# Attention scores from block-diagonal keys, the pass flag ahead of the gather, and a reordered last group of down steps, in a one-core Trainium2 step of a hybrid decoder layer

## What is computed

```python
def token_mix(x, ...):
    h = rmsnorm(x, g_mix)
    mq, mk, mv, mo, mi, mf, aq, ak, av = split_in(h @ w_in)
    # 4 mLSTM heads (256 x 256 memory), and 16 query heads on 4 key heads of 64,
    # sliding window of 128, with a sink per head
    return x + concatenate([o_m, o_a]) @ w_out, states

def sink_attention(q, k, v, allowed, sinks):
    s = einsum('...thgd,...khd->...hgtk', q, k) * 64 ** -0.5
    s = where(allowed, s, -inf)
    mx = maximum(max(s), sink)
    e = exp(s - mx)
    p = e / (sum(e) + exp(sink - mx))
    return einsum('...hgtk,...khd->...thgd', p, v)

def channel_mix(x, p_i, ...):
    # top-1 of 4 groups, top-2 of 8 experts in it, 32 SwiGLU experts of 512
    x = x + hier_moe(rmsnorm(x, g_ffn), ...)
    gate = sigmoid(rmsnorm(x, g_ple) @ w_ple_gate)
    return x + gate * (p_i @ w_ple_proj)
```

## Time and profile before, and how to read it

| what | us |
|---|---|
| median of 3 executions | 1517.54 |
| lowest, highest | 1515.83, 1518.03 |
| profiled execution, its own time | 1517.73 |
| its span | 1516.0 |
| PE busy | 1364.2 (90%) |
| weight loads busy | 859.7 (57%) |
| DVE, ACT, POOL busy | 350.8, 252.4, 31.4 |
| DMA, mean | 348 GB/s |

### The profile page before, as it was taken

The page is one execution under the profiler, slowest core; times in us unless marked ns, Lnnn a source line. Parts: engine busy times, 40 slices in busy tenths (PEclk is TensorE's granted clock), DMA queues, the critical chain, the costliest instruction groups (busy, mean ns, idle before and its releaser), DMA issues.

```text
span 1516.0 us, 22808 instructions
## 1 busy us (share of the span) xinstructions
PE 1364.2 (90%) x9764; PEld 859.7 (57%) x9765; DVE 350.8 (23%) x938; ACT 252.4 (17%) x558; POOL 31.4 (2%) x69
## 2 busy tenths in 40 slices
PE   9989999999999999987978787888788888999986
PEld 7878888888888543433523333333333356666655
DVE  3312221036621411301301010101010112222217
ACT  3201121041401322111101111110111111101015
POOL 1000000020022000000000000000000000000000
PEclk9999999999999999989989899899998999999998
DMA  9556333377978699999999999999999999999981
GB/s 343 204 169 227 118 132 113 138 279 264 375 291 371 268 427 401 426 427 428 426 427 428 428 429 429 428 429 428 428 429 428 429 413 427 426 426 428 427 345 58
DMA packets 64640, 527.50 MB, mean 348 GB/s; under 512 B 6030, under 2 KB 27926, under 8 KB 29350
## 3 DMA queue, kind: packets, MB, share of 16 engines
q1 hardware_dynamic: 63182, 525.27, 84.5%
q10 hardware_dynamic: 1384, 1.16, 0.2%
HBM read 512.33 MB, written 14.07 MB: 347 GB/s over the span
## 4 chain that ended last, share of the span: by engine, by line
DMA 42%; PE 26%; DVE 1%; issue 1%; ACT 1%; DVEq 0%; ACTq 0%
DMA raw<-in_w_up 26%; DMA more<-in_w_up 8%; PE ps L1944 7%; DMA raw<-in_w_down_cuts 7%; PE ps L2208 4%; PE ps L2182 4%; PE ps L154 4%; DMA more<-in_w_down_cuts 1%; PE ps L2192 1%; PE ps L1184 1%; PE ps L1968 1%; PE ps L1919 1%; PE ps L1957 1%; PE ps L1260 1%; PE ps L1239 0%
## 5 line engine op out<-in xcount | busy, mean ns | idle before, releaser
L154 PE MATMUL ps<-mixT_hT,raw 128*128 128x264 f32 x1920 | 436.1, 387 | 2.3 <-PEq L808 1.7
L154 PEld LDWEIGHTS ps<-mixT_hT,raw 128*128 128x128 f32 x1920 | 361.9, 190 | 67.1 <-issue 6.9
L1944 PE MATMUL ps<-raw,mixT_hT 128*32 128x512 f32 x1488 | 200.2, 669 | 90.7 <-DMA raw<-in_w_up 62.0
L1944 PEld LDWEIGHTS ps<-raw,mixT_hT 128*32 128x32 f32 x1488 | 43.0, 116 | 212.6 <-DMA raw<-in_w_up 88.3
L2208 PE MATMUL ps<-mixT_hT,more 128*128 128x264 f32 x512 | 126.1, 395 | 1.2 <-ACT mixT_hT L2289 1.2
L1199 DVE TENSOR_TENSOR mixT_hT<-ps,ffn_gain 128x512 f32<-128x512 f32 x33 | 22.8, 691 | 417.9 <-PE ps L1919 417.9
L2208 PEld LDWEIGHTS ps<-mixT_hT,more 128*128 128x128 f32 x512 | 94.9, 191 | 30.8 <-issue 16.4
L1184 PE MATMUL ps<-x_res,mine 128*32 128x512 f32 (+1 forms) x792 | 109.0, 668 | 0.0
L1957 PEld LDWEIGHTS ps<-fold,mixT_hT 128*128 128x128 f32 x512 | 69.3, 210 | 53.6 <-issue 35.2
L1919 PEld LDWEIGHTS ps<-ident,xe 128*64 128x64 f32 x1056 | 66.5, 217 | 28.3 <-issue 28.3
L1957 PE MATMUL ps<-fold,mixT_hT 128*128 128x32 f32 x512 | 76.6, 296 | 5.7 <-ACT mixT_hT L1766 5.7
(11 more groups left out here) (373 smaller groups left out, 905.5 us busy)
## 6 DMA issues: line engine op xcount, KB each, us to landing
raw<-in_w_gate SPq DMA_DIRECT2D x62, 2048.0 KB, 16.5
raw<-in_w_down_cuts SPq DMA_DIRECT2D x35, 2048.0 KB, 17.5
more<-in_w_up SPq DMA_DIRECT2D x32, 2048.0 KB, 15.4
raw<-in_w_up SPq DMA_DIRECT2D x31, 2048.0 KB, 16.9
raw<-in_mix_chunks SPq DMA_DIRECT2D x60, 1024.0 KB, 5.4
more<-in_w_down SPq DMA_DIRECT2D x16, 2048.0 KB, 22.4
more<-in_w_down_cuts SPq DMA_DIRECT2D x13, 2048.0 KB, 25.6
more<-in_w_gate_cuts SPq DMA_DIRECT2D x8, 2048.0 KB, 21.6
```

Of the source, the lines that this page charges most:

```text
L154: return nc.tensor.matmul(ps[:, j, 0:NT], core.raw[:, q % NCH, k * GW + j * P:k * GW + (j + 1) * P], xT[:, core.groups[g].k0 + c * CK + k, ...
L1944: last = nc.tensor.matmul(ps[own, (GATE, UP)[m], :], xT[:, k, i * SLOTS:(i + 1) * SLOTS], weights, start=(i == 0 and k < 4), stop=(i == EI ...
```

## The change

In attention, `kswp` gives way to `both_keys`, two buffers (for even and odd `g`) of two rows of blocks: the keys of one key head in the upper 64 partitions with zeros below, and the same keys in the lower 64 with zeros above. One product of 128 rows takes the queries of two heads as weights and both key blocks as 2 x 128 or 2 x 256 columns; its output holds the scores of both heads. Two products per unit replace four. POOL clears the zero halves behind its other work (four memsets) and signals `a_clear`; DVE copies the keys of head 0 and 1 at the start and those of 2 and 3 behind units 1 and 3 (`group_keys`). PE waits for `a_clear` ahead of all scores, and for `a_keys` in each unit. In the routing, the sums for the flag (`before`) are made ahead of DVE's wait for the ranks, PE's counting product goes ahead of the gather and into bank 6, both pieces of `state(3, b)` go behind the gather, and the flag is made right behind `mine`. In finish_stage step 5 follows the order of the others, and `most_total` comes behind the last block.

```diff
-    kswp = S("kswp", [P, 2, NT])
+    both_keys = S("both_keys", [P, 2, 2, SEQ])
...
             pool.sem_inc(q["a_const"], 1)
+            for i in range(2):
+                link(nc.gpsimd.memset(both_keys[HD:P, i, 0, :], 0.0))
+                link(nc.gpsimd.memset(both_keys[0:HD, i, 1, :], 0.0))
+            pool.sem_inc(q["a_clear"], 1)
...
-            pe.wait_ge(q["a_swap"], 2)
+            pe.wait_ge(q["a_clear"], 1)
             pe.wait_ge(q["a_rows"], 2)
...
-                for i in range(4):
-                    h = 4 * g + i
-                    lo = (h % 2) * HD
-                    keys = pT[lo:lo + HD, AK0 + g // 2, 0:span(b)] if h % 2 == g % 2 else kswp[lo:lo + HD, g // 2, 0:span(b)]
-                    last = nc.tensor.matmul(ps[:, 4 + i % 2, (i // 2) * 256:(i // 2) * 256 + span(b)],
-                                            pT[lo:lo + HD, AQ0 + h // 2, b * P:(b + 1) * P], keys,
+                pe.wait_ge(q["a_keys"], 2 * g + 2)
+                for a in range(2):
+                    out = ps[:, 4 + a, :].rearrange("p (i c) -> p i c", i=2)[:, :, 0:span(b)]
+                    last = nc.tensor.matmul(out, pT[:, AQ0 + 2 * g + a, b * P:(b + 1) * P], both_keys[:, g % 2, :, 0:span(b)],
                                             start=True, stop=True)
...
-            nc.vector.tensor_copy(kswp[0:HD], pT[HD:P, AK0:AK0 + 2, :]).then_inc(q["a_swap"], 1)
-            nc.vector.tensor_copy(kswp[HD:P], pT[0:HD, AK0:AK0 + 2, :]).then_inc(q["a_swap"], 1)
+            def group_keys(g):
+                if g >= 2:
+                    dve.wait_ge(q["a_scores"], 2 * g - 2)
+                src = pT[g % 2 * HD:(g % 2 + 1) * HD, AK0 + g // 2, 0:SEQ]
+                for half in range(2):
+                    nc.vector.tensor_copy(both_keys[half * HD:(half + 1) * HD, g % 2, half, :], src).then_inc(q["a_keys"], 1)
+
+            group_keys(0)
+            group_keys(1)
...
                 if u % 2:
                     projected(u // 2)
+                    if u < 5:
+                        group_keys(u // 2 + 2)
...
+        pe.wait_ge(q["r_before"], 1)
+        nc.tensor.matmul(ps[:, 6, 0:NE], core.ones[:], before[:, 2, :], start=True, stop=True).then_inc(q["r_counted"], 1)
+        gather_slots(core, pe, rt, shared, 0)
         state(3, 0)
-        gather_slots(core, pe, rt, shared, 0)
         state(3, 1)
-        pe.wait_ge(q["r_before"], 1)
-        nc.tensor.matmul(ps[:, 0, 2 * P:2 * P + NE], core.ones[:], before[:, 2, :], start=True, stop=True).then_inc(q["r_counted"], 1)
...
+        dve.wait_ge(q["r_counted"], 1)
+        link(V.tensor_reduce(c[:, 8, 0:1], ps[:, 6, 0:NE], AX, ALU.max))
+        V.tensor_tensor(rt["flag"][:], c[0:1, 8, 0:1].to_broadcast([1, PASSES]), rt["level"][0:1, :], ALU.is_gt
+                        ).then_inc(shared["flag_ready"], 1)
...
-                elif j == GROUPS - 1:
-                    gates(c - 1, j)
-                    if c == LAST:
-                        most_total()
-                    down(c, j)
-                    sums(c, j)
                 else:
                     down(c, j)
                     gates(c - 1, j)
                     sums(c, j)
+        most_total()
```

More of the change, by code:

```diff
@@ L493, in attention @@
     st = S("st", [P, 4, NS])
-    names = ("a_const a_swap a_rows a_rowsT a_sinks a_win a_new a_stored a_scores a_shift a_exp "
+    names = ("a_const a_clear a_keys a_rows a_rowsT a_sinks a_win a_new a_stored a_scores a_shift a_exp "
              "a_prob a_turn a_turned a_pv a_mixed a_bias s_sinks s_q s_keysT s_kcopy s_scores s_shift s_exp s_turn "
@@ L726, in _ @@
                     src = ps[:, 4 + a, :].rearrange("p (i c) -> p i c", i=2)[:, :, 0:span(b)]
-                    nc.vector.scalar_tensor_tensor(sm[:, u % 2, a::2, 0:span(b)], src, HD ** -0.5, msk, ALU.mult, ALU.add
+                    nc.vector.scalar_tensor_tensor(sm[:, u % 2, 2 * a:2 * a + 2, 0:span(b)], src, HD ** -0.5, msk, ALU.mult, ALU.add
                                                    ).then_inc(q["a_shift"], 1)
@@ L1614, in vector @@
         link(V.tensor_tensor(c[:, 9, :], rt["pick_r"][:, 0:3, 0], rt["pick_r"][:, 3:6, 0], ALU.add))
+        link(V.tensor_tensor(before[:, 1, :], both[:, 0, :], both[:, 1, :], ALU.add))
+        link(V.scalar_tensor_tensor(before[:, 2, :], both[:, 2, :], valid[:], before[:, 1, :], ALU.mult, ALU.add))
+        dve.sem_inc(q["r_before"], 1)
         dve.wait_ge(q["r_ranked"], 1)
@@ L1620, in vector @@
         dve.sem_inc(shared["pick_step"], 1)
+        dve.wait_ge(q["r_counted"], 1)
+        link(V.tensor_reduce(c[:, 8, 0:1], ps[:, 6, 0:NE], AX, ALU.max))
+        V.tensor_tensor(rt["flag"][:], c[0:1, 8, 0:1].to_broadcast([1, PASSES]), rt["level"][0:1, :], ALU.is_gt
+                        ).then_inc(shared["flag_ready"], 1)
         ranks = ps[:, 0, P:P + 3 * NE].rearrange("p (o e) -> p o e", o=1).to_broadcast([P, 2, 3 * NE])
         link(V.tensor_tensor(taken.rearrange("p (i t) e -> p i (t e)", i=2), ranks, pick[:].rearrange("p i t e -> p i (t e)"), ALU.mult))
-        link(V.tensor_tensor(before[:, 1, :], both[:, 0, :], both[:, 1, :], ALU.add))
-        link(V.scalar_tensor_tensor(before[:, 2, :], both[:, 2, :], valid[:], before[:, 1, :], ALU.mult, ALU.add))
-        dve.sem_inc(q["r_before"], 1)
         link(V.tensor_reduce(rt["rank"][:], taken, AX, ALU.add))
@@ L1629, in vector @@
         V.tensor_tensor(c[:, 5, :], c[:, 4, :], c[:, 3, :], ALU.subtract).then_inc(q["r_in2"], 1)
[L1630 to L1633, removed]
         dve.wait_ge(shared["gain_landed"], 16)
```

## The result

The changed kernel took 1527.76 us (median of six, 1524.97 to 1530.83) against 1517.34 us (median of six) for the kernel before: a ratio of 1.007, 95% interval 1.006 to 1.008. It is 10.4 us slower. The forecast was 1519.5 us and its range ended at 1523.0, so it was wrong. The profiled execution took 1530.83 us, the slowest of the six, with a span of 1528.4 us against 1516.0, 12.4 more.

The account below looks back on a forecast made before the run. Prediction: DMA loads of expert weights bound the kernel from 574 us on; PE counts before that and after the last landing. Terms 3.8 + 0 + 1.4 - 0.8 - 2.0 - 0.4 = +2.0 us gave 1519.5 us, range 1516.5 to 1523.0.

Parts of the forecast that it names:

- Between 574 and 1464 us PE's time is hidden: From the restart of the weight-load stream to the last down step, PE's gains or losses do not move the end.
- a dry stretch of the stream behind 580 us: Sign of a wrong forecast: the load stream, expected full until the last down step, runs dry after 580 us.
- The price of the attention units, +3.8: Attention scores: two products of 512 columns replace four paired ones and cost 3.8 us more, bounds +3.2 and +4.4.
- Rival 3: Attention scores: half-zero products cost no more than paired halves and the drains go, 1.6 us gained, 1514.1 us; chance 0.07.
- Start of the stage, 0 and +1.4: Attention start: PE's wait for the clearing costs 0, the clock falling behind that idle time costs 1.4 us.
- Rival 2: Attention start: the clock holds behind the wait, so 1.4 us less, 1518.1 us; chance 0.17.
- Routing tail, -0.8: Routing tail: the flag's load runs beside the queued state products, so x_turn starts 0.8 us sooner.
- Clock in the routing, -2.0: Routing tail: without the 1.4 us hole the clock does not fall, 2.0 us gained, bounds 0 and -2.1.
- rival 1: Routing tail gives nothing back: flag load waits for state products, or the clock falls all the same; 1522.3 us, chance 0.20.
- End, -0.4: Last block: down ahead of gates lets the sums and everything behind them come 0.4 us sooner, bounds -0.7 and +0.5.

Follow-up runs that it names:

- e1: Changed kernel plus 25 TensorE instructions in a branch that is not run, moving the finish's code back; 1521.78 us, ratio to the kernel before 1.0039.
- e7: As e1, with the four clearings of the key tile ahead of the mask on GpSimd; 1520.00 us, ratio to the kernel before 1.0018.
- e8: Changed kernel without its attention part, so routing and finish only; 1515.80 us against 1517.25 for the kernel before, ratio 0.9994.
- e9: The kernel of e8 measured once more, nothing changed; 1516.70 us against 1517.87 for the kernel before, ratio 0.9994.
- e3: Attention part of the change alone on the kernel before; 1526.67 us, ratio 1.0069.
- e6: Changed kernel plus 8 TensorE instructions in the branch that is not run; 1528.49 us (one run).
- e5: Kernel before plus 199 TensorE instructions in the branch that is not run; 1524.11 us against 1517.25, ratio 1.0038.
- e10: Kernel of e8 with the branch for further passes left out of TensorE's program; 1515.56 us against 1517.87 for the kernel before, ratio 0.9986.
- e4: Routing part of the change alone on the kernel before; 1516.34 us, ratio 0.9996.

## Why the prediction was wrong, point by point

By medians: the place of the code 6.0 us (after less e1), the wait for the clearing with its clock 1.8 (e1 less e7), the block-diagonal units 3.8 (e7's 1520.00 less 1516.25, the middle of e8 and e9), routing and finish -1.3 (middle of e8 and e9). Together 10.3, where 10.4 were measured; since each term is the step from one kernel to the next, the sum is no test of them. The split is good to about 1 us: by means of the runs, each less the kernel before measured beside it, it is 4.8, 2.5, 4.2 and -1.1. The prediction had 0, 1.4, 3.8 and -3.2.

- **"Between 574 and 1464 us PE's time is hidden" is the step that failed.** It was read from a DMA share that stays full in the kernel before. The share says that no stop empties the stream now; it doesn't say how much more it bears. What the runs show in its place is +8.89 us in just this stretch, from a second stop that the prediction had no term for, since it never asked where the finish's code would lie. Its own sign of being wrong, a dry stretch of the stream behind 580 us, is what came (DMA share 0.30 from 1230 to 1235 us). TensorE already stood still for 4.87 us at 1213 us. From the restart to the first product of the finish, 643.1 us pass in e3 and 643.4 in e6, and the second stop costs 3.3 and 3.4 us of the stream's piece; in the changed kernel and e5 it is 647.1 and 647.2 us, and it costs 8.9 and 8.7. That being late raises the price fits these four executions and is not shown apart from them. Without a second stop 645.1 us cost nothing in e1 (877.91); e7, e8 and e9 took 1.7 to 2 us more in this piece (879.95, 879.70, 879.70), and that stays open. In the changed kernel part of the lateness is a stretch at half clock (0.62 and 0.69 in the windows 1205 to 1210 and 1210 to 1215 us).
- **The price of the attention units, +3.8: right.** The traces give 3.58, and 3.6 to 3.7 in all five kernels with this part; a unit with two key blocks takes 1.82 us, forecast 1.7 to 1.8. Rival 3 (a half-empty product costs no more) is out: the columns account for the price.
- **Start of the stage, 0 and +1.4: right in sum, by another split.** The clearing was done at 103.85 us, earlier than the 104.1 forecast, and the clock fell as feared. The first turn came 1.22 us later in this execution, 2.66 in e1's. Rival 2 (the clock holds) fell. In e7, with a wait of 1.67 us, it would have been right; in e10 the clock fell behind 1.50 us, so the wait alone doesn't decide it.
- **Routing tail, -0.8: the mechanism is right.** The register load does overlap: x_turn starts at 526.19, as the state's products end (524.27 + 1.99), where the earlier trace rows have 1.43 us of idle time ahead of it. The size is right too: at full clock the piece is 0.8 us shorter (134.8 against 135.61).
- **Clock in the routing, -2.0: mis-sized.** The first expert had its full clock (5.36 us), but the fall came earlier and hit the gather (4.55 in place of 2.91 us). The claim was that without the 1.4 us hole the clock would hold. It held in e5 with that hole (1.44 us) and fell in e4 without it. Over the kernels with the new routing the piece from 436 to 574 us takes 134.8 to 139.8 us (mean of eight 136.5); with the old one 135.6 to 137.6 (mean of four 137.0). So routing gave 0.5 us on the mean where 2.8 were forecast. That was the second half of rival 1.
- **End, -0.4: right where it was aimed, gone behind it.** The sums start 2.86 us behind the landing of the down weights (1464.2 + 16.7 = 1480.9), against 3.27 before. But the gate tile then waits for its own weights (1464.6 + 22.4 = 1487.0), so 0.14 us is left in this trace, and the same piece varies from 63.12 to 64.69 us over the kernels with the new order.

## What to carry to other kernels

A change of instruction count moves all code behind it, and that can cost as much as the change itself: if TensorE stops with "issue" behind a loop or a jump, shift the code by instructions in a branch that isn't taken before blaming the change, and try both kernels that way. If that happens, look for packets on the instruction queue in the stops. A stream that is full in a profile has a reserve, not an endless one; before counting an engine's time as hidden, add up the stops that it already has there. Put clearings ahead of other set-up work that nobody waits for yet.

## What the runs showed of the hardware

TensorE stopped for 4.3 to 5.1 us at two kinds of places that no semaphore explains: behind a jump over code that isn't run (gone in e10), and at a fixed place in the code reached about 15 instructions behind such a jump (e3, e5, e6 and the changed kernel). In the second case 8 instructions of shift moved it by 8 instructions, and a shift of 256 (by the count) brought it back. Each stop ends 1.7 or 1.4 us behind the landing of a 16 KB packet on the instruction queue, one of which comes for 256 of TensorE's records; the second comes 5.7 to 6.0 us behind the first whether TensorE waits for it or not. And a product of 128 contraction rows with half of them zero has the price of its columns: 1.82 us for the four records of 512, where eight paired ones of 256 take 1.06.
